# Ten input-projection panels by seven block products instead of eight, with x parked in DRAM

## What is computed

```python
u = rmsnorm(x, ng[1]) * (1.0 + sc2) + sh2
proj = u @ P['w_in'][l]                      # 1024 -> 2816
p_conv, p_rwkv, p_pool, p_sb = jnp.split(proj, IN_SPLITS, axis=-1)
q, k, v = jnp.split(p_sb, 3, axis=-1)        # per-head norm on q and k
y_d = sb_attention(q, k_all, v_all, pos0, sb_bias)
...
x = x + g2 * (merged @ P['w_out'][l])
```

## Time and profile before

| what | us |
|---|---|
| median of 3 runs | 3203.75 |
| lowest, highest | 3203.20, 3205.34 |
| the profiled execution, its own time | 3207.98 |
| its span in the trace | 3206.3 |
| TensorE matmul busy | 3135.1 (98%) |
| VectorE busy | 1168.5 (36%) |
| GpSimd busy | 853.2 (27%) |
| ScalarE busy | 469.4 (15%) |
| mean granted TensorE clock | 0.994 |

### The profile page before, as it was taken

One profiled execution on the slowest core, in us unless ns is written; L12 is line 12 of the kernel. 1 busy time (PEld: TensorE's weight loads), 2 busy tenths in 40 slices (PEclk: granted clock), 3 DMA queues, 4 the chain that ended last, 5 costly groups with the idle time before them and its releaser, 6 DMA issues.

```text
span 3206.3 us, 42657 instructions
## 1 busy us (share of the span) xinstructions
PE 3135.1 (98%) x17664; PEld 2482.4 (77%) x17664; DVE 1168.5 (36%) x2229; ACT 469.4 (15%) x844; POOL 853.2 (27%) x741
## 2 busy tenths in 40 slices
PE   7999999999999999999989999999999999999998
PEld 4777887677777878888867778876777778788887
DVE  3223422353233463344232233224533244533432
ACT  2000002313111120000020000034031111200100
POOL 2333430110000334444333333302100003344442
PEclk9999999999999999999999999999999999999999
DMA  6444322441111222222254442224311113122221
GB/s 266 178 164 184 112 86 92 141 140 39 50 51 58 89 77 81 79 81 84 87 224 166 163 184 99 86 93 145 125 53 50 36 56 111 70 79 79 89 73 64
DMA packets 72288, 335.34 MB, mean 105 GB/s; under 512 B 10400, under 2 KB 27552, under 8 KB 38944
## 3 DMA queue, kind: packets, MB, share of 16 engines
q1 hardware_dynamic: 63360, 312.03, 26.9%
q0 software_dynamic: 6176, 16.79, 1.7%
q10 hardware_dynamic: 2560, 3.80, 0.3%
HBM read 326.55 MB, written 6.02 MB: 104 GB/s over the span
## 4 chain that ended last, share of the span: by engine, by line
PE 93%; ACT 2%; DVE 2%; DMA 1%; issue 0%; SPq 0%; DVEq 0%; ACTq 0%
PE ps L662 93%; ACT ws L1390 1%; DVE ws L1661 1%; ACT L1390 1%; DMA ring<-w_up 1%; DMA lp<-params 0%; DVE ws L1664 0%; DVE proj L1661 0%; DMA ring<-w_ada 0%; DVE x L1664 0%; ACT proj L1390 0%; DVE masked_room L2032 0%; PE ps L717 0%; PE ps L1217 0%; DVE u L1661 0%
## 5 line engine op out<-in xcount | busy, mean ns | idle before, releaser
L662 PE MATMUL ps<-u,ring 128*128 128x272 f32 x4608 | 1156.5, 401 | 27.1 <-ACT u L1390 18.8
L662 PEld LDWEIGHTS ps<-u,ring 128*128 128x128 f32 x4608 | 866.9, 192 | 245.4 <-issue 53.7
L1661 DVE TENSOR_TENSOR ws<-ws,ps 128x272 f32<-128x272 f32 (+2 forms) x778 | 347.2, 452 | 1479.8 <-PE ps L662 1469.9
L631 POOL TENSOR_TENSOR masked_room<-ring 128x512 f32<-128x512 f32 (+1 forms) x76 | 95.9, 1262 | 1315.5 <-DVE pause L2358 659.4
L662 PE MATMUL ps<-y,ring 128*128 128x272 f32 x1376 | 350.8, 393 | 0.0
L1390 ACT ACTIVATE ws<-ps 128x272 f32<-128x272 f32 (+1 forms) x398 | 154.9, 396 | 1312.3 <-PE ps L662 1312.0
L662 PE MATMUL ps<-y,masked_room 128*128 128x272 f32 x1296 | 315.8, 393 | 2.8 <-DVE ws L1661 2.8
L662 PE MATMUL ps<-y,ws 128*128 128x272 f32 x1296 | 315.6, 393 | 0.0
L662 PEld LDWEIGHTS ps<-y,ring 128*128 128x128 f32 x1376 | 261.3, 190 | 54.4 <-DVE proj L1661 0.7
L662 PEld LDWEIGHTS ps<-y,masked_room 128*128 128x128 f32 x1296 | 245.7, 190 | 55.5 <-issue 4.8
L662 PEld LDWEIGHTS ps<-y,ws 128*128 128x128 f32 x1296 | 245.9, 190 | 52.0 <-issue 1.5
(11 more groups left out here) (195 smaller groups left out, 2557.9 us busy)
## 6 DMA issues: line engine op xcount, KB each, us to landing
ring<-w_up SPq DMA_DIRECT2D x88, 1024.0 KB, 4.8
ring<-w_ada SPq DMA_DIRECT2D x72, 1024.0 KB, 4.9
ring<-w_down SPq DMA_DIRECT2D x32, 1024.0 KB, 4.8
ring<-w_gate SPq DMA_DIRECT2D x32, 1024.0 KB, 4.8
ring<-w_in SPq DMA_DIRECT2D x22, 1024.0 KB, 4.8
ws<-cache SPq DMA_DIRECT2D x128, 128.0 KB, 3.1
ws<-cache POOLq DMA_DIRECT2D x128, 128.0 KB, 3.4
ring<-w_down SPq DMA_DIRECT2D x16, 768.0 KB, 4.1
```

Of the source, the lines that this page charges most:

```text
L631: nc.gpsimd.tensor_tensor(sums[:, 0], a21, a22, ALU.add).then_inc(w_sums.sem, 1)
L662: return nc.tensor.matmul(out, lhsT, rhs, start=start, stop=stop, skip_group_check=skip)
L1661: return V.tensor_tensor(out, a, b, op)
```

## The change

Panel 0 stays as it was: units 0 to 3. Panels 1 to 10 are each done as seven products of 4 matmuls, "units" 4 to 73, in the order M1, M6, M2, M7, M5, M4, M3. Unit n uses bank 4 + n % 2 and may start when unit n - 2 is out. VectorE adds each product directly to the places in `proj` where the outputs belong: seven instructions for a panel instead of four. GpSimd forms three weight sums for each panel, one of them in place in the ring, and the fourth in place once M2 is done. The token sums (four of 128x1088) take the room of x, and the weight sums take room in `y` and `proj`; so x is stored to DRAM in four parts by ScalarE's queue, three during the first down projection and one in the norm, and loaded again by GpSimd's queue after the last unit; the output projection waits for it. The places of the halves in the program remain, translated by `in_units`: halves 13 and 14 become units 20 to 22, 15 and 16 units 23 to 26, 3h+17 becomes two units, 3h+18 and 3h+19 three units (29 to 31, 34 to 36, 39 to 41), a panel after a turn of cache values seven.

```diff
+IN_UNITS = 4 + 7 * 10
...
+def in_units(half):
+    return half if half <= 4 else 4 + (7 * (half - 4) + 2) // 4
...
-k = 4 * n + 4
+k = 4 + 7 * n
...
+x_room = nc.dram_tensor("x_room", (P, KT, T), F32).ap()
+in_tsum = x[:, :, :].rearrange("p a (b n) -> p (a b) n", n=HALF).rearrange("p (s k) n -> p s k n", s=4)
+def in_wsum(panel):
+    tiles = {7: proj[:, 12:14, :], 8: proj[:, 14:16, :], 9: proj[:, 18:20, :], 10: proj[:, 20:22, :]}
+    room = tiles[panel] if panel in tiles else y[:, 2 * (1 - panel % 2):2 * (1 - panel % 2) + 2, :]
+    return room.rearrange("p a n -> p (a n)")[:, 0:1024].rearrange("p (s k m) -> p s k m", s=2, k=4)
...
+        def in_three_sums(panel):
+            a11, a12, a21, a22 = in_blocks(panel)
+            sums, at = in_wsum(panel), 3 * (panel - 1)
+            if panel > 2:
+                pool.wait_ge(part.sem, part.upto(l, PART0["in"] + in_unit(panel - 2, "M7") + 1))
+            if panel > 8:
+                pool.wait_ge(kv_stored.sem, kv_stored.upto(l, 2))
+            nc.gpsimd.tensor_tensor(sums[:, 1], a11, a21, ALU.subtract).then_inc(in_three.sem, 1)
+            pool.wait_ge(in_three.sem, in_three.upto(l, at + 1))
+            nc.gpsimd.tensor_tensor(a21, a21, a22, ALU.add).then_inc(in_three.sem, 1)
+            pool.wait_ge(in_three.sem, in_three.upto(l, at + 2))
+            nc.gpsimd.tensor_tensor(sums[:, 0], a21, a11, ALU.subtract).then_inc(in_three.sem, 1)
+        def in_fourth_sum(panel):
+            a11, a12, a21, a22 = in_blocks(panel)
+            pool.wait_ge(part.sem, part.upto(l, PART0["in"] + in_unit(panel, "M2") + 1))
+            pool.wait_ge(in_three.sem, in_three.upto(l, 3 * panel))
+            nc.gpsimd.tensor_tensor(a12, a12, in_wsum(panel)[:, 0], ALU.subtract).then_inc(in_fourth.sem, 1)
...
         pool.wait_ge(x_done.sem, x_done.upto(l, 8))
-        cache_loads(0, 32)
+        in_three_sums(1)
+        cache_loads(0, 4)
+        pool.wait_ge(in_tok.sem, in_tok.upto(l, 4))
+        in_three_sums(2)
+        for panel in (1, 2):
+            in_fourth_sum(panel)
+            in_three_sums(panel + 2)
+        in_fourth_sum(3)
+        in_three_sums(5)
+        cache_loads(4, 8)
+        in_fourth_sum(4)
+        in_three_sums(6)
+        cache_loads(8, 12)
+        in_fourth_sum(5)
+        cache_loads(12, 16)
+        in_three_sums(7)
+        for panel in (6, 7, 8):
+            cache_loads(4 * panel - 8, 4 * panel - 4)
+            in_fourth_sum(panel)
+            in_three_sums(panel + 2)
+        cache_loads(28, 32)
+        in_fourth_sum(9)
+        in_fourth_sum(10)
+        pool.wait_ge(part.sem, part.upto(l, PART0["in"] + IN_UNITS))
+        pool.wait_ge(x_kept.sem, x_kept.upto(l, 4))
+        pool.dma_start(x[:, :, :], x_room).then_inc(x_back.sem, 16)
...
+            for unit in range(in_units(a), in_units(b)):
+                half(unit) if unit < 4 else block(unit)
+        def block(unit):
+            j, i = 1 + (unit - 4) // 7, (unit - 4) % 7
+            s, sums = load_number(l, "in", j) % R, in_wsum(j)
+            if i == 0:
+                panel(l, "in", j)
+            def w(k, c):
+                return ring[:, s, k * 256 + c * P:k * 256 + c * P + P]
+            pe_.wait_ge(in_done.sem, in_done.upto(l, unit - 1))
+            if i in (1, 3, 4):
+                pe_.wait_ge(in_three.sem, in_three.upto(l, 3 * j))
+            if i == 6:
+                pe_.wait_ge(in_fourth.sem, in_fourth.upto(l, j))
+            if j == 1 and i in (1, 3, 4, 5):
+                pe_.wait_ge(in_tok.sem, in_tok.upto(l, (0, 2, 0, 3, 3, 4)[i]))
+            for k in range(4):
+                left, right = ((w(k, 0), u[:, k, 0:HALF]), (sums[:, 0, k, :], in_tsum[:, 1, k, :]),
+                               (w(4 + k, 0), u[:, 4 + k, 0:HALF]), (sums[:, 1, k, :], in_tsum[:, 2, k, :]),
+                               (w(k, 1), in_tsum[:, 0, k, :]), (w(4 + k, 1), in_tsum[:, 3, k, :]),
+                               (w(4 + k, 0), u[:, 4 + k, HALF:T]))[i]
+                m = mm(ps[:, 4 + unit % 2, 0:HALF], left, right, start=i in (0, 1, 4) and k == 0, stop=k == 3,
+                       skip=True)
+            m.then_inc(part.sem, 1)
...
+            if d == 0 and p < 3:
+                keep_x(l, p)
+    def keep_x(l, p):
+        if p == 0:
+            act.wait_ge(x_back.sem, x_back.upto(l, 0))
+        act.dma_start(x_room[:, 2 * p:2 * p + 2, :], x[:, 2 * p:2 * p + 2, :]).then_inc(x_kept.sem, 16)
...
+        if n == 1:
+            keep_x(l, 3)
...
+            if d == 1 and p == 0:
+                dve.wait_ge(x_back.sem, x_back.upto(l, 1))
...
+        for unit in range(in_units(a), in_units(b)):
+            dve.wait_ge(part.sem, part.upto(l, PART0["in"] + unit + 1))
+            got = ps[:, 4 + unit % 2, 0:HALF]
+            if unit < 4:
...
+                j, i = 1 + (unit - 4) // 7, (unit - 4) % 7
+                c11, c12 = (proj[:, 2 * IN_ORDER[j], hf * HALF:hf * HALF + HALF] for hf in range(2))
+                c21, c22 = (proj[:, 2 * IN_ORDER[j] + 1, hf * HALF:hf * HALF + HALF] for hf in range(2))
+                if i in (1, 4, 6):
+                    dve.wait_ge(in_done.sem, in_done.upto(l, unit))
+                if i == 0:
+                    m = V.tensor_copy(c21, got)
+                if i == 1:
+                    m = tt_(c12, c21, got, ADD)
+                if i == 2:
+                    m = V.tensor_copy(c11, got)
+                if i == 3:
+                    m = tt_(c22, c21, got, ADD)
+                if i == 4:
+                    m = tt_(c22, c22, got, ADD)
+                if i == 5:
+                    m = tt_(c21, c21, got, ADD)
+                if i == 6:
+                    m = tt_(c12, c12, got, ADD)
+            m.then_inc(in_done.sem, 1)
...
+    def in_token_sum(l, i):
+        b11, b12, b21, b22 = u[:, 0:4, 0:HALF], u[:, 0:4, HALF:T], u[:, 4:8, 0:HALF], u[:, 4:8, HALF:T]
+        if i == 0:
+            dve.wait_ge(x_kept.sem, x_kept.upto(l, 4))
+            dve.wait_ge(up_done.sem, up_done.upto(l, U0[1] + 16))
+            dve.wait_ge(us_done.sem, us_done.upto(l, 2))
+            tt_(in_tsum[:, 0], b12, b11, SUB).then_inc(in_tok.sem, 1)
+        elif i == 1:
+            dve.wait_ge(in_tok.sem, in_tok.upto(l, 1))
+            tt_(in_tsum[:, 1], b22, in_tsum[:, 0], SUB).then_inc(in_tok.sem, 1)
+        elif i == 2:
+            tt_(in_tsum[:, 2], b22, b12, SUB).then_inc(in_tok.sem, 1)
+        else:
+            dve.wait_ge(in_tok.sem, in_tok.upto(l, 2))
+            tt_(in_tsum[:, 3], b21, in_tsum[:, 1], SUB).then_inc(in_tok.sem, 1)
...
         evict(l, 0, 2)
+        in_token_sum(l, 0)
+        in_token_sum(l, 1)
+        evict(l, 2, 3)
+        in_token_sum(l, 2)
         keep_modulation(l, 8)
-        evict(l, 2, 12)
+        evict(l, 3, 4)
+        in_token_sum(l, 3)
+        evict(l, 4, 12)
```

More of the change, by code:

```diff
@@ L158 @@
 SEVEN_CHUNKS = (DOWN_CHUNKS, ((0, 4),), DOWN_CHUNKS)
+IN_UNITS = 4 + 7 * 10
 STAGES = [("ada", ADA_FIRST, ADA_FIRST), ("up0", FT + ADA_UP, FT + ADA_UP),
-          ("down0", DOWN, DOWN), ("in", 11, 44), ("gate", 24, 2 * FILLS), ("gate_b", 8, 8),
+          ("down0", DOWN, DOWN), ("in", 11, IN_UNITS), ("gate", 24, 2 * FILLS), ("gate_b", 8, 8),
           ("out", 4, 4), ("up1", FT, FT), ("down1", DOWN, DOWN)]
@@ L199, in in_half, with in_unit @@
     return (j, c, hf) if j else (j, hf, c)
+def in_units(half):
+    return half if half <= 4 else 4 + (7 * (half - 4) + 2) // 4
+def in_unit(panel, name):
+    return 4 + 7 * (panel - 1) + ("M1", "M6", "M2", "M7", "M5", "M4", "M3").index(name)
 def last_part(stage, n):
@@ L468, in build @@
         o_sums = signal("merged_sums", 4)
+        in_tok = signal("projection_token_sums", 4)
+        in_three = signal("projection_three_weight_sums", 3 * 10)
+        in_fourth = signal("projection_fourth_weight_sum", 10)
+        x_kept = signal("x_stored_for_later", 4, unit=16)
+        x_back = signal("x_loaded_again", 1, unit=16)
         branch_pe = signal("last_branch_products", 4)
@@ L475, in build @@
         x_done = signal("x_tiles", 24, credit=2)
-        in_done = signal("proj_halves", 44)
+        in_done = signal("projection_outputs", IN_UNITS)
         merge_done = signal("merged", 8)
@@ L646, in weight_sums, with in_blocks @@
                         block_sums(f"down{f}", i, unit_of(f"down{f}", i), DOWN_CHUNKS[i % 3][1])
+                def in_blocks(panel):
+                    slot = panel_wait(pool, l, "in", panel)
+                    w = ring[:, slot, :].rearrange("p (k m) -> p k m", k=KT)
+                    return w[:, 0:4, 0:P], w[:, 4:8, 0:P], w[:, 0:4, P:256], w[:, 4:8, P:256]
+                def in_three_sums(panel):
[10 more added lines that the diff above has]
+                    nc.gpsimd.tensor_tensor(sums[:, 0], a21, a11, ALU.subtract).then_inc(in_three.sem, 1)
@@ L945, in halves_in, with half @@
                 def halves_in(a, b):
-                    for n in range(a, b):
+                    for unit in range(in_units(a), in_units(b)):
```

(17 more changed lines are left out.)

2 lines of the change are left out of this document (1 added, 1 removed).

## The result

| | before | after |
|---|---|---|
| median of 4 runs beside each other, us | 3204.43 | 3263.77 |
| lowest, highest | 3203.20, 3205.34 | 3255.52, 3266.39 |
| ratio, 95% interval | | 1.018 [1.016, 1.020] |
| the profiled execution, its own time | 3207.98 | 3263.24 |
| its span | 3206.3 | 3261.6 |

The change makes the kernel 1.8% slower. Forecast were 3234 us and a range of 3208 to 3258: the direction is right, the size is not, and the time lies outside the range. The executions of one kernel scatter by up to 11 us (3255.52 to 3266.39 here), so a difference of a few us between two medians is rough; the waits in the traces repeat to the hundredth.

The account below looks back on a forecast made before the run. It took TensorE's work plus its idle time as the bound. Net waits of 9.4 us, clock 20.7 and store 0.4 summed to 30.5 us slower, 3234.3 us for the median, with a range of 3208 to 3258.

Parts of the forecast that it names:

- Removed work: Input projection on TensorE: 40 fewer matmuls a layer, ten products' time, 18.3 us saved a layer, 36.7 in both.
- (a): Units 29 to 31, 34 to 36, 39 to 41: third product idles 5.1 us behind the softplus; 14.6 us a layer.
- (b): Units 23 to 26: TensorE idles 3.8 us until the eviction behind `softplus(0)`.
- (c): Units 20 to 22: TensorE idles 3.3 us until VectorE evicts behind the norm of Q and K.
- Port: VectorE instructions with two SBUF inputs held by GpSimd's weight sums beside the attention: taken as 0, at most 10 us in all.
- (d): Panels 7 to 10: late evictions in the pooling (about 0.9 us) and behind the token shift (about 0.4), together 1.3 us.
- The clock: TensorE at half speed after long waits: 4.5 falls a layer, 2.3 us lost in each, 20.7 us in both layers.
- What was costed at nothing: Token sums, evictions not late, weight sums in GpSimd's queue: nothing; store of x 0.4 us in all, reload covered.
- The rival with GpSimd as the bound: GpSimd late at three panels, 18 us, and port 10: 30.5 + 28, giving 3262 us; chance 0.1.
- The rival "faster": Softplus back in under 3.8 us, before two products are done, so no third product waits: 3177 us; chance 0.07.

Follow-up runs that it names:

- the fitted kernel: The e7 kernel with GpSimd's weight sums placed by hand into stretches in which VectorE waits; 3192.01 us, ratio 0.9957.
- e1: Kernel after, with VectorE evicting the first two units of each softplus hole ahead of the softplus instead of behind it; 3232.06 us, ratio 1.008.
- e5: Kernel after, with only panel 5's three weight sums moved behind panel 4's fourth sum; 3255.55 us, ratio 1.015.
- e2: Kernel after, with GpSimd's weight sums formed over one column of each block instead of 128, outputs not the model's; 3239.40 us, ratio 1.010.
- e10: The fitted kernel without the `in_units` edit, so heads' units shared as in the kernel after, panel 5's fourth sum a step earlier; 3204.12 us, ratio 0.9996.
- e3: Kernel after, with unused matmuls run in TensorE's waits ahead of units 22, 25, 31, 36 and 41; 3241.37 us, ratio 1.011.
- e4: Kernel after, without the stores of x, its reload and the waits on them, outputs not the model's; 3263.80 us, ratio 1.018.
- e7: Kernel after, with early evictions, panel 5's sums moved, heads' units shared otherwise, unit 20 evicted before the norm, finer later evictions; 3215.74 us, ratio 1.0026.
- e8: The run of the fitted kernel: e7 with four waits a layer added to GpSimd's queue and its sums and page loads reordered; 3192.01 us, ratio 0.9957.

## Why the prediction was wrong, and where it was right

**Removed work**: 18.3 us a layer, right: 160 records fewer, and 32.8 of the 36.7 us come out as less busy time in the fitted kernel.

**(a) and (b)**: right to a tenth. 5.04 in each of three heads (forecast 5.1), 3.79 (3.8), released by evictions, and e1 showed the mechanism by taking it away.

**(c)**, 3.3 forecast, 6.29 measured. The order of VectorE was right, and without the sums beside it the wait is 3.37. The step of the prediction that failed is "Port. ... I take 0": the sums of panel 5 ran beside the norm of Q and K, whose two long multiplies took 3.64 us for 2.61 and the eight small copies 2.74 for 0.82. The forecast looked for collisions only in the path of (a), where indeed none lengthens a wait in this kernel, and never laid the start of each group of sums beside what VectorE does at that time. That costs 2.9 us of waiting a layer, and in all, by the medians of e5, some 8 us.

**(d)**, 1.3 forecast, 5.2 and 5.9 measured (3.41 and 1.82; 3.41 and 2.45). The same failed step: beside the sums for panels 9 and 10 some operations of the pooling are held until a sum ends, and four of the convolution with 512 columns take 4.56 us (1.73 for four without sums). With tiny sums one wait of 0.85 is left, ahead of unit 52, as forecast. The 0.4 ahead of unit 66 never came. All in all the port term is about 24 us (e2), against a bound of 10, which counted four places a layer at 1.27 us: it had neither the chains of operations, which can be held again by the next sum, nor the clock behind the waits that this makes longer.

The Trainium skill, SBUF — State Buffer, section "Who interferes with whom", says that of a VectorE instruction with two SBUF inputs and a GpSimd instruction that reads SBUF the second waits for the whole of the first. The runs agree: 1.04 and 1.25 us for operations of 0.16 and 0.18, beside sums of 1.27 and 1.66, and ending with them. The eight copies at (c), 2.74 us for 0.82, have one input each, so the rule as quoted does not cover them; they were held all the same. The forecast quoted the rule, and its sentence that the sum would be up to 10 us higher by it had the right direction and less than half of the size.

**Head 3's values**, 0.15 before, 1.99 after, not forecast. `in_units` rounds, and the pause of head 2 holds four units, 39 to 42, not the three that were written ahead of the prediction; for head 3 one unit is left where one half stood, 1.8 us less cover. With two units there the wait is 0.15 in layer 0 of the fitted kernel, with one again it is 1.99 (e10). The formula was in the diff, and it was not worked out for all of its places.

**The clock**, 20.7 forecast, 26.8 measured. (a), (b) and (c) have their fall in both layers, (c) too, because it became longer; that part, by e3, is 22.4. Of the other 4.4 us one fall, 2.7 us by the stretches of 706 to 714, stands at the wait of 3.41 in layer 0, in a place where the forecast had under 1 us of wait; the remaining 1.7 are not placed. The forecast argued from four long waits of the kernel before with a fall at each. The same trace has two falls without a wait: at 1012 to 1014 us, and again at 2600 to 2602, TensorE had been busy for all of the 12 us before, the last of them with rows of small matmuls (64x8 and 32x32):

```profile
1012.00:1014.00 2.00, 2.00 (x6) 1.42 (x6) 0.83 (x3) 0.00 (x0) 0.00 (x0) 0.50 0.00 0
```

So the term is 6.1 us too small because ten falls came where nine were counted, and because of the 4.4 us elsewhere. The size of one fall was right, 2.2 against 2.3.

**What was costed at nothing** and was nothing: token sums, evictions by number, the traffic of x (e4), GpSimd's queue. The rival with GpSimd as the bound named 3262, and nearly that came out, by luck: half of it was GpSimd late at three panels, and no wait of TensorE is released by GpSimd; the sums hold VectorE up instead.

**The range** ended at 3258 because half of the port's bound was taken into it. With 24.4 in the place of that 10 the same formula reaches 3265 and holds the time.

**The rival "faster"** asked for a softplus back within 3.8 us, and that did not come: in the kernel after VectorE waits the same 7.85 us ahead of it. But products do fill the waits once VectorE evicts ahead of the softplus (31.7 us less alone), the sums are fitted (23.7 less than in e7), and the pauses hold four units (12.1, e8 against e10). These three are differences from different kernels and do not add up to one sum.

## What to carry to other kernels

Work that is cut into smaller pieces needs its consumer to come back as much more often. With a fixed number of banks, go through every stretch in which the consumer is tied up longer than the banks' worth of products, before counting what the pieces save. Work moved to GpSimd is to be laid on the clock beside VectorE's, start by start: here its cost was decided by what VectorE did at that moment, and a wait added to GpSimd's queue can be the cheapest edit there is. And an edit that balances one resource is to be tried with the others mended as well as alone, since its sign can depend on them.

## What the runs showed of the hardware that was not expected

- Waits far below those of the earlier trace rows can be followed by a fall of the clock: 2.07 us (PEclk 0.53 behind it), 1.75 us (0.64), and in the fitted kernel two of 0.96 and 1.06 us close together (0.57 from 654 to 658 us). Others of the same length are not: behind 1.99 and 1.82 us in the kernel after PEclk is 1.00, and a wait of 3.41 us is followed by 0.50 in layer 0 and 1.00 in layer 1. And it can fall with no wait at all, as at 1012 us of the kernel before. No run here says what decides between them. Behind the 0.68 us of the fitted kernel, six times, it did not fall; for one of them:

```profile
602.00:610.00 8.00, 8.00 (x41) 4.18 (x40) 1.64 (x2) 2.55 (x3) 3.81 (x3) 1.00 0.21 66
```

- A VectorE operation of 16 columns can be held until a weight sum of 512 columns on GpSimd that it meets has ended, and both sides are held: in the kernel after such sums take up to 2.19 us for 1.27.
- 98 more matmuls whose results nobody reads made the kernel 22.4 us faster, by holding the clock through ten waits.
